# Branch A's attention scores: three pairs of 64-row matmuls over half the array, or four 128-row matmuls over stacked high and low parts

## The reference, cut to what matters

```python
s = einsum('bqhmd,bkhmd->bhmqk', qb, k) * scale + bias   # per head h and map m
s = where(mask, s, NEG_INF)                              # chunk-causal
p = softmax(s, axis=-1)
attn = p[:, :, 0] - lam * p[:, :, 1]
o = einsum('bhqk,bkhe->bqhe', attn, v)
```

## Time and profile before

| what | value |
|---|---|
| median of 3 runs | 1826.25 us (1825.3, 1826.25, 3576.29) |
| profiled execution, own time | 1823.93 us |
| its span | 1822.1 us |
| PE busy | 1783.3 us (98%), 9007 matmuls |
| DVE busy | 1048.4 us (58%) |
| ACT busy | 701.6 us (39%) |
| POOL busy | 661.9 us (36%) |
| 69 to 533 us (heads 0 to 7 of branch A), 464 us | PE 456.76, DVE 297.82, ACT 243.57, POOL 77.20 us |

### The profile page before, as it was taken

The page is one execution under the profiler, slowest core; times in us unless marked ns, Lnnn a source line. Parts: engine busy times, 40 slices in busy tenths (PEclk is TensorE's granted clock), DMA queues, the critical chain, the costliest instruction groups (busy, mean ns, idle before and its releaser), DMA issues.

```text
span 1822.1 us, 25660 instructions
## 1 busy us (share of the span) xinstructions
PE 1783.3 (98%) x9007; PEld 1453.0 (80%) x9007; DVE 1048.4 (58%) x2291; ACT 701.6 (39%) x1544; POOL 661.9 (36%) x662
## 2 busy tenths in 40 slices
PE   5999999999999999999999999999999999999998
PEld 4777777777778888888888878788888888888886
DVE  5366666656665554111432565677766666777767
ACT  5355555555556666310222132322223333222232
POOL 4311112111123444322222250465555656655560
PEclk9999999999999999999999999999999999999999
DMA  6411111111111101134322440121121111111112
GB/s 239 140 35 33 49 36 36 47 34 35 44 34 43 33 24 36 46 81 160 103 83 91 140 153 0 59 69 46 46 69 46 46 46 46 56 59 46 60 45 92
DMA packets 143398, 117.91 MB, mean 65 GB/s; under 512 B 23556, under 2 KB 130252, under 8 KB 143308
## 3 DMA queue, kind: packets, MB, share of 16 engines
q1 hardware_dynamic: 134092, 112.52, 20.1%
q10 hardware_dynamic: 9216, 4.20, 0.8%
HBM read 99.88 MB, written 21.53 MB: 67 GB/s over the span
## 4 chain that ended last, share of the span: by engine, by line
PE 88%; DVE 4%; ACT 3%; POOL 3%; issue 2%; DMA 0%; SPq 0%; ACTq 0%; DVEq 0%; POOLq 0%
PE bank L569 27%; PE bank L571 26%; PE bank L570 26%; PE bank L607 4%; PE bank L595 3%; PE bank L655 2%; POOL w_lo L1190 1%; ACT mix L971 1%; DVE mix L1476 1%; DVE mix L1455 1%; POOL hT_lo L1207 1%; PE bank L656 1%; DVE y_lo L1329 0%; ACT w_hi L862 0%; ACT mix L1025 0%
## 5 line engine op out<-in xcount | busy, mean ns | idle before, releaser
L569 PE MATMUL bank<-hT_hi,w_hi 128*128 128x512 f32 x1312 | 528.0, 402 | 9.0 <-POOL hT_lo L1207 5.9
L571 PE MATMUL bank<-hT_hi,w_lo 128*128 128x512 f32 x1312 | 512.3, 390 | 0.0
L570 PE MATMUL bank<-hT_lo,w_hi 128*128 128x512 f32 x1312 | 512.3, 390 | 0.0
L1190 POOL TENSOR_TENSOR w_lo<-w_raw,w_hi 128x256 fp32r<-128x256 f32 x264 | 189.3, 748 | 616.9 <-ACT w_hi L862 616.9
L569 PEld LDWEIGHTS bank<-hT_hi,w_hi 128*128 128x128 f32 x1312 | 246.5, 188 | 82.7 <-issue 16.7
L571 PEld LDWEIGHTS bank<-hT_hi,w_lo 128*128 128x128 f32 x1312 | 246.7, 188 | 53.6
L570 PEld LDWEIGHTS bank<-hT_lo,w_hi 128*128 128x128 f32 x1312 | 247.1, 188 | 46.2
L569 PE MATMUL bank<-y_hi 128*128 128x512 f32 (+1 forms) x548 | 205.9, 376 | 0.8 <-issue 0.8
L570 PE MATMUL bank<-y_lo,y_hi 128*128 128x512 f32 (+1 forms) x548 | 203.3, 371 | 0.0
L571 PE MATMUL bank<-y_hi,y_lo 128*128 128x512 f32 (+1 forms) x548 | 203.2, 371 | 0.0
L1271 POOL TENSOR_TENSOR y_lo<-y_full,y_hi 128x512 fp32r<-128x512 f32 x98 | 131.8, 1377 | 165.6 <-ACT y_hi L1125 165.6
(11 more groups left out here) (172 smaller groups left out, 2856.9 us busy)
## 6 DMA issues: line engine op xcount, KB each, us to landing
w_raw<-in_w_in_dram SPq DMA_DIRECT2D x100, 256.0 KB, 3.3
w_raw<-in_w_ff_dram SPq DMA_DIRECT2D x64, 256.0 KB, 4.1
y_full<-in_w_ff_dram SPq DMA_DIRECT2D x32, 512.0 KB, 3.7
bias_rows<-bias_line SPq DMA_DIRECT2D x3, 1536.0 KB
res<-in_x_dram SPq DMA_DIRECT2D x8, 512.0 KB, 6.3
x_spill<-res SPq DMA_DIRECT2D x8, 512.0 KB, 5.9
o_spill<-o_buf ACTq DMA_DIRECT2D x64, 64.0 KB, 1.6
w_raw<-in_w_branch_b_dram SPq DMA_DIRECT2D x16, 256.0 KB, 3.9
```

What stands on the lines that cost most here:

```text
L569: pe.matmul(bank, lhs[0], rhs[0], start=start, stop=False)
L570: pe.matmul(bank, lhs[0], rhs[1], start=False, stop=False)
L571: return pe.matmul(bank, lhs[1], rhs[0], start=False, stop=stop)
L1190: ins = pool.tensor_tensor(w[1][:, n % 2, at:at + 2], w_raw[:, at:at + 2, :], w[0][:, n % 2, at:at + 2].bitcast(F32), ALU.subtract)
```

## The change

Branch A's scores of one map are now two 128-row matmuls instead of three 64-row ones. For each map, q's high part is written twice, into rows 0 to 63 and into rows 64 to 127 of one tile; the other tile has q's low part in the map's own 64 rows and zeros in the other 64. k's high and low parts of one map are stacked: high in the map's own rows, low in the other 64. (q_hi, q_hi) times (k_hi, k_lo) gives hi*hi + hi*lo, and (q_lo, 0) times the same gives lo*hi. The odd heads' q tiles get memory of their own (`q_odd`, in `res`). POOL zeroes the unused halves, once for each parity. `scores` stays for branch B alone.

```diff
@@ -153,9 +153,14 @@
         unused = sb("unused", [P, P])
 
 
-        q = [t[:, 0:2, :] for t in y]
-        k = [t[:, 2:4, :] for t in y]
-
+        k_b = [t[:, 2, :] for t in y]
+
+
+
+        ROWS = (slice(0, HD), slice(HD, P))
+        q_odd = [nc.alloc_sbuf_tensor_at(f"q_odd{i}", [P, 2, SEQ], F32R, offset=y_at + (4 * KT + 2 + 2 * i) * SEQ * 4) for i in range(2)]
+        q_a = [[[t[:, m, :] for t in pair] for m in range(2)] for pair in (y, q_odd)]
+        k_a = [[t[:, 2 + slot, :] for t in y] for slot in range(2)]
         v_a = y[0][:, 4:6, :].rearrange("p s (t r e) -> p (s t) r e", r=2, e=P)
         v_main = [t[:, 4:6, :].rearrange("p s k -> p (s k)")[:, 0:NT * 192].rearrange("p (t c) -> p t c", t=NT) for t in y]
         v_side = [t[:, 7, :].rearrange("p (t c) -> p t c", t=NT) for t in y]
@@ -241,6 +246,7 @@
         freed_act = sem("freed_act")
         freed_dve = sem("freed_dve")
         qk_hi = sem("qk_hi")
+        q_zero = sem("q_zero")
         tr_done = sem("tr_done")
         tr_hi = sem("tr_hi")
         tr_lo = sem("tr_lo")
@@ -595,8 +601,7 @@
                     mm = pe.transpose(TR[n % 2][:, at * P:(at + 1) * P], src, ident[:, :])
                 mm.then_inc(tr_done, 1)
 
-            def scores(units, k_slot, pieces):
-
+            def scores(units, pieces):
 
                 if units[1] >= 3:
                     pe.wait_ge(scores_read, units[1] - 2)
@@ -605,7 +610,7 @@
                         for m in range(2):
                             rows = slice(m * HD, (m + 1) * HD)
                             mm = pe.matmul(SC[units[m] % 3][:, at:at + keys.stop - keys.start], queries[left][rows],
-                                           k[right][rows, k_slot, keys], start=not (left or right), stop=left == 1)
+                                           k_b[right][rows, keys], start=not (left or right), stop=left == 1)
                             if left == 1 and at == pieces[-1][2]:
                                 mm.then_inc(scores_done, 1)
 
@@ -662,8 +667,15 @@
                     if i == 0:
                         pe.wait_ge(freed_dve, freed(False, LAST[TILE[("ka", h)]]))
                     def block_a(c):
-                        scores([SCORE[("a", h, i, m, c)] for m in range(2)], h % 2,
-                               [([t[:, h % 2, i * P:(i + 1) * P] for t in q], slice(c * HALF, min((c + 1) * HALF, (i + 1) * P)), 0)])
+                        keys = slice(c * HALF, min((c + 1) * HALF, (i + 1) * P))
+                        for m in range(2):
+                            unit = SCORE[("a", h, i, m, c)]
+                            if unit >= 3:
+                                pe.wait_ge(scores_read, unit - 2)
+                            for part in range(2):
+                                mm = pe.matmul(SC[unit % 3][:, 0:keys.stop - keys.start], q_a[h % 2][m][part][:, i * P:(i + 1) * P],
+                                               k_a[h % 2][m][:, keys], start=part == 0, stop=part == 1)
+                            mm.then_inc(scores_done, 1)
 
                     block_a(0)
                     step = h * NT + i
@@ -691,7 +703,7 @@
                 half, at = i // 4, i % 4 * P
                 if i % 4 == 0:
                     pe.wait_ge(freed_dve, freed(False, POS[(TILE[("qb", 2 * g + 1)], half)]))
-                scores([SCORE[("b", g, i, m, 0)] for m in range(2)], 0,
+                scores([SCORE[("b", g, i, m, 0)] for m in range(2)],
                        [([t[:, half, j, at:at + P] for t in q_b], slice(i * P - CHUNK if i else 0, (i + 1) * P), j * 192 + (0 if i else CHUNK))
                         for j in range(2)])
 
@@ -876,11 +888,18 @@
                 cols = slice(half * HALF, (half + 1) * HALF)
                 src = GEMM[g % 2][:, :]
                 if kind == "qa":
-                    act.activation(q[0][:, h % 2, cols], src, ACT.Copy, scale=SCALE).then_inc(qk_hi, 1)
+                    for m in range(2):
+                        for rows in ROWS:
+                            ins = act.activation(q_a[h % 2][m][0][rows, cols], src[ROWS[m]], ACT.Copy, scale=SCALE)
+                    ins.then_inc(qk_hi, 1)
+                elif kind == "ka":
+                    for m in range(2):
+                        ins = act.activation(k_a[h % 2][m][ROWS[m], cols], src[ROWS[m]], ACT.Copy)
+                    ins.then_inc(qk_hi, 1)
                 elif kind == "qb":
                     act.activation(q_b[0][:, half, h % 2, :], src, ACT.Copy, scale=SCALE).then_inc(qk_hi, 1)
-                elif kind in ("ka", "kb"):
-                    act.activation(k[0][:, h % 2, cols], src, ACT.Copy).then_inc(qk_hi, 1)
+                elif kind == "kb":
+                    act.activation(k_b[0][:, cols], src, ACT.Copy).then_inc(qk_hi, 1)
                 elif kind in ("va", "vb"):
                     act.activation(vT[:, cols], src, ACT.Copy).then_inc(freed_act, 1)
                 else:
@@ -1198,6 +1217,12 @@
                 pool.tensor_copy(bias_a[:, slot, 0:SEQ - 2 * P], bias_a[:, slot, SEQ - 2 * P:SEQ - 2 * P + 1].broadcast_to([P, SEQ - 2 * P])).then_inc(bias_ready, 1)
 
             pool.memset(eps, EPS).then_inc(eps_ready, 1)
+
+            def zero_rows(pair):
+                for m in range(2):
+                    pool.memset(pair[m][1].bitcast(F32), 0.0).then_inc(q_zero, 1)
+
+            zero_rows(q_a[0])
             split_weights(0)
             for n in range(2 * KT):
                 kt, cols = n % KT, slice(n // KT * HALF, (n // KT + 1) * HALF)
@@ -1212,6 +1237,9 @@
                 kind, i = TILES[n]
                 if kind == "qa" and i >= 1 or n == 2:
                     bias_a_rest(i)
+                if n == 2:
+                    pool.wait_ge(spilled, 16 * NT)
+                    zero_rows(q_a[1])
 
             def set_sink(s):
 
@@ -1337,11 +1365,19 @@
                 g = POS[(n, half)]
                 dve.wait_ge(qk_hi, count_of(("qa", "ka", "kb", "qb"), g))
                 cols = slice(half * HALF, (half + 1) * HALF)
+                bank = GEMM[g % 2]
                 if kind == "qb":
-                    hi, lo = (t[:, half, h % 2, :] for t in q_b)
+                    pieces = [[t[:, half, h % 2, :] for t in q_b] + [bank[:, :]]]
+                elif kind == "kb":
+                    pieces = [[t[:, cols] for t in k_b] + [bank[:, :]]]
+                elif kind == "qa":
+                    dve.wait_ge(q_zero, 2 * (h % 2 + 1))
+                    pieces = [[t[ROWS[m], cols] for t in q_a[h % 2][m]] + [bank[ROWS[m], :]] for m in range(2)]
                 else:
-                    hi, lo = (t[:, h % 2, cols] for t in (q if kind == "qa" else k))
-                dve.scalar_tensor_tensor(lo, GEMM[g % 2][:, :], 1.0 if kind in ("ka", "kb") else SCALE, hi.bitcast(F32), ALU.mult, ALU.subtract).then_inc(freed_dve, 1)
+                    pieces = [[k_a[h % 2][m][rows, cols] for rows in (ROWS[m], ROWS[1 - m])] + [bank[ROWS[m], :]] for m in range(2)]
+                for hi, lo, src in pieces:
+                    ins = dve.scalar_tensor_tensor(lo, src, 1.0 if kind in ("ka", "kb") else SCALE, hi.bitcast(F32), ALU.mult, ALU.subtract)
+                ins.then_inc(freed_dve, 1)
 
             def moments(n, t):
```

## The result

| kernel | median | ratio to before |
|---|---|---|
| before, on the same chip | 1825.78 us | 1 |
| changed | 1867.95 us (fastest 1866.31) | 1.0232, 95% [1.0218, 1.0246] |

The change costs 42 us, 2.3%. The forecast was 1854, its range ended at 1866. One of the four runs of the changed kernel (2016.26 us, granted clock 0.846) and one of before (3576.29) were disturbed and stand outside the ratio. The profiled execution took 1866.31 us, its span 1863.6.

A forecast was written before the change was run, and what follows sets the result against it. PE was taken as the bound (88% of the chain), with the DVE and ACT chain having no slack. 1823.9 + 23.1 (branch A) + 1.8 (start) + 4 (clock) = 1852.8 us, stated as 1854; range 1832 to 1866.

The forecast's parts named there:

- PE's part: Branch A's score blocks: 0.2 us less for each of 12 blocks a head, 19 us for eight heads if nothing else held PE.
- the weight tile: PE's step 5 wait for the weight tile takes back what that step's two blocks save: +0.45 us a head.
- R1: Rival: the chain over DVE and ACT has hidden slack, no wait in step 4: -14 us, 1810 us; chance 0.06.
- R4: Rival: stacked matmuls miss one spacing as weight loads show, up to 0.1 us for each of 384: 1870 us; chance 0.02.
- Two new waits, at their places: PE waits in heads 0 to 6: about 1.5 us before step 1's fifth v transpose, some 4.1 at step 4's second block.
- R2: Rival: 64-row instructions on ACT and DVE cost half: about -6 us, 1818 us; chance 0.07.
- The price of a piece: Each added 64-row instruction costs 0.50 us on ACT, 0.60 on DVE: q half +2.1, k half +1.1, 5.3 us a head.
- the slack: At step 4's second score block: 0.32 plus 0.13 us, so PE passes 5.3 - 0.45 = 4.85 us later.
- the first head's share: Head 0 has no former head's output rows in step 1, some 1.1 us less chain: +2.6 us instead of +3.7.
- The start: Before branch A: first k copy +1.1 us, second q copy 0.7, memsets 0 (at most 4): +1.8 us.
- The clock: Branch A: the granted clock may fall after the 4 us wait in seven heads: 4 us taken, between 0 and 12.
- R3: Rival: the clock falls at every wait, unhidden, 7 to 14 falls x 1.7 us: 1861 to 1873 us; chance 0.11.

The follow-up runs named there:

- experiment 1: Kernel before with its own three matmul pairs, plus the change's 64-row copies and low parts on ACT and DVE for heads 1 to 7: 1882.25 us, ratio 1.0320.
- experiment 3: Changed kernel with each copy and low part of heads 1 to 7 reading and writing rows 0 to 63: 1859.38 us in its one run.
- experiment 9: Changed kernel with head 0's q and k copied and completed by one 128-row instruction each, as before the change: 1863.44 us, ratio 1.0214.
- experiment 5: Changed kernel with useless matmuls of 512 columns ahead of both waits, 14 in step 4 and 8 in step 1: 1862.03 us, ratio 1.0208.
- experiment 2: Changed kernel with its stacked matmuls, but q and k copied and completed by one 128-row instruction: 1811.23 us, ratio 0.9926.

## Why the prediction failed, point by point

**PE's part: right.** 0.91 us a block with no gaps, and 14.4 us gained alone in branch A, 13 in the time, where 19 less 3.6 for the weight tile had been worked out (R1's sum). R4 falls with it.

**Two new waits, at their places: right.** Both at the instruction named, in each of seven heads (at step 1 of head 0 an old wait grew), and experiment 1 shows the same two with the old matmuls. R1 (slack) falls: it expected no wait at step 4. R2 (half price for half the rows) falls as well: a piece of 64 rows takes what one of 128 does (0.59 against 0.60 us).

**The price of a piece: this is the step that failed.** "I take 0.50 and 0.60, because the instructions of these rows grow with columns while all 128 rows go at once." That holds for instructions that start at the same row. The pieces alternate between row 0 and row 64, and then each waits for the one before to finish: 0.61 and 0.71. By the prediction's own steps, q half +2.8 instead of 2.1 and k half +0.6 x 2 - 0.5 + 0.7 x 2 - 0.6 = 1.5 instead of 1.1, the chain of a head is 7.1 instead of 5.3 us. All of it lies past the slack: 1.8 us a head.

Measured at full clock, a head of the changed kernel is 40.05 + 23.10 = 63.15 us from one wait of step 4 to the next, against 58.2 between the same places before (330.31 to 388.46 in the trace): +4.95, where +3.7 was predicted. With all pieces at row 0 (experiment 3) it is 39.47 + 21.99 = 61.46, so +3.3. The alternating start row is thus 1.7 us a head, as the corrected prices say, and the prediction's other terms together came out 0.4 a head too high: luck, in the direction that hid a part of the error. Over branch A, without the clock's part, 36.3 - 5 = 31 us are lost where 23.1 was worked out: about 8 more, 1.25 a head and the first head's share. The lengths in experiment 3 rest on one trace.

**The start: mis-sized.** 1.8 predicted; 3.3 to 4.5 measured in the time by experiment 9. The 4.5 us of the two profiles are 1.7 that were there before any piece had run (35.42 against 33.71 us) and 2.8 behind it. I priced the first k half alone, as the one that lies on the chain, and 0.7 for the second q half. The first q half counts too: from its copy to the k copy it is 9.6 to 9.7 us in the four profiles with pieces in the old order and 8.2 to 9.2 without. From the k copy on it is 30.1 against 27.4 to 27.7, so 2.4 us or more. In the profiles with pieces PE also waits 1.0 us and more for the third weight tile (63.64 us), and in none without; how much of the loss is that wait's was not taken apart. The four memsets cost nothing that any view shows.

**The clock: nearly right.** 4 predicted (0 to 12), 4.4 to 5.9 measured by experiment 5. R3 was right that a wait of either length can be followed by a fall (nine falls, within its 7 to 14), and wrong about the price: it took each fall in full, 1.7 us. Four of the nine, behind step 1, cost nothing, and the five behind step 4 cost 1.1 each; why these do not cost their full 1.7 was not taken apart.

**The sum.** 8 (branch A, the pieces' price) + 1.5 to 2.7 (start) + 0.4 to 1.9 (clock) + 0.7 (the rest) = 11 to 13 us, of the 14 by which 1854 was short.

## What to carry to other kernels

When an edit cuts one instruction in several, price each at its full duration, not at its spacing, unless all start at the same row; and add the engines up where one waits for the other's last piece. Then ask what is queued behind them: here the pieces cost 57 us (the changed kernel less experiment 2), and 53 of them were not the work but its place, and a different order gave them back. A change on the bound engine can be right and still lose; run its two halves apart before judging it.

## What was not expected of the hardware

- ACT, too, loses its overlap when start rows alternate: 0.61 us from start to start for copies of 64 rows by 512 columns, 0.48 when all start at row 0. DVE: 0.71 against 0.60.
- PE waits of 1.9 to 4.8 us between stretches of dense matmuls were followed by a fall from 2.4 to 1.2 GHz nine times in fourteen, and the length of the wait did not tell which (1.88 us was, 3.69 was not). What the falls cost in time was a third of what they took from the clock: a fall that ends before PE's next wait for a chain of other engines comes off that wait (23.09 us with it, 23.10 without).
